# New orders at the ends of parts in a chain of two transformer blocks, and a conditioning product that ends eight blocks earlier

## The reference

```python
m_lat = jnp.split(cond_lat @ ada_w[i] + ada_b[i], 6, axis=-1)
h_lat = layer_norm(ALPHA * h_lat + m_lat[2] * y_lat, ln_g[i, 0], ln_b[i, 0])
f_lat = swiglu_2(modulate(h_lat, m_lat[3], m_lat[4]), ffn_w13[i], ffn_w2[i])
h_lat = layer_norm(ALPHA * h_lat + m_lat[5] * f_lat, ln_g[i, 1], ln_b[i, 1])
```

## Time and profile before

| | |
|---|---|
| Median of 3 runs | 2839.1 us (2837.92 to 2840.66) |
| The profiled execution: its own time | 2836.78 us |
| Its span, first to last instruction | 2835.0 us |
| Mean granted TensorE clock | 0.997 of full |
| PE busy | 2790.1 us, 98% |
| DVE busy | 1750.8 us, 62% |
| ACT, POOL busy | 1173.3 us (41%), 502.2 us (18%) |
| HBM read | 261.49 MB, 93 GB/s over the span |

### The profile page before, as it was taken

The page is one execution under the profiler, slowest core; times in us unless marked ns, Lnnn a source line. Parts: engine busy times, 40 slices in busy tenths (PEclk is TensorE's granted clock), DMA queues, the critical chain, the costliest instruction groups (busy, mean ns, idle before and its releaser), DMA issues.

```text
span 2835.0 us, 40815 instructions
## 1 busy us (share of the span) xinstructions
PE 2790.1 (98%) x16006; PEld 2449.7 (86%) x16006; DVE 1750.8 (62%) x3061; ACT 1173.3 (41%) x2064; POOL 502.2 (18%) x272
## 2 busy tenths in 40 slices
PE   9999999999999999999999999999999999999998
PEld 8888896988889888888888989999997778988888
DVE  7778688758795653544445896556675535633344
ACT  5332358642233641422424743334345555532222
POOL 2243300023332101111111000000012222122220
PEclk9999999999999999999999999999999999999999
DMA  6556412236654211121021012222223121133331
GB/s 207 183 186 193 148 63 90 75 110 218 187 193 124 83 45 60 38 67 45 31 86 48 17 62 76 71 68 64 79 68 101 49 75 66 53 112 104 97 97 38
DMA packets 86015, 267.81 MB, mean 94 GB/s; under 512 B 9152, under 2 KB 18752, under 8 KB 85568
## 3 DMA queue, kind: packets, MB, share of 16 engines
q1 hardware_dynamic: 85824, 265.20, 29.2%
HBM read 261.49 MB, written 2.10 MB: 93 GB/s over the span
## 4 chain that ended last, share of the span: by engine, by line
PE 92%; DVE 5%; ACT 1%; issue 1%; DMA 1%; SPq 0%; POOL 0%; DVEq 0%; ACTq 0%
PE ps L1986 29%; PE ps L1988 29%; PE ps L1987 29%; PE ps L2261 1%; PE ps L2245 1%; PE ps L2234 1%; DVE t_wlo L2661 1%; DMA t_x<-in_x 0%; PE ps L2125 0%; ACT t_whi L2303 0%; PE ps L2117 0%; PE ps L2176 0%; DVE t_m L2778 0%; PE ps L2189 0%; DVE t_hid L2905 0%
## 5 line engine op out<-in xcount | busy, mean ns | idle before, releaser
L1986 PE MATMUL ps<-t_h,t_whi 128*128 128x512 f32 (+2 forms) x2040 | 710.9, 348 | 3.6 <-DVE t_m L2980 1.3
L1987 PE MATMUL ps<-t_h,t_wlo 128*128 128x512 f32 (+2 forms) x2040 | 705.9, 346 | 0.0
L1988 PE MATMUL ps<-t_h,t_whi 128*128 128x512 f32 (+2 forms) x2040 | 705.7, 346 | 0.0
L2303 ACT CAST t_whi<-t_raw 128x1024 fp32r<-128x1024 f32 (+3 forms) x405 | 351.7, 875 | 580.5 <-PE ps L1988 446.3
L3272 POOL TENSOR_TENSOR t_wlo<-t_raw,t_whi 128x1024 fp32r<-128x1024 f32 (+3 forms) x130 | 292.6, 2251 | 1534.6 <-ACT t_whi L2303 1534.6
L1986 PE MATMUL ps<-t_hid,t_whi 128*128 128x256 f32 (+2 forms) x1336 | 436.1, 326 | 11.5 <-DVE t_hid L2711 6.1
L1987 PE MATMUL ps<-t_hid,t_wlo 128*128 128x256 f32 (+2 forms) x1336 | 433.1, 324 | 0.0
L1988 PE MATMUL ps<-t_hid,t_whi 128*128 128x256 f32 (+2 forms) x1336 | 432.5, 324 | 0.0
L1986 PEld LDWEIGHTS ps<-t_h,t_whi 128*128 128x128 f32 x2040 | 385.6, 189 | 51.7 <-issue 8.2
L1987 PEld LDWEIGHTS ps<-t_h,t_wlo 128*128 128x128 f32 x2040 | 385.7, 189 | 42.5 <-issue 1.2
L1988 PEld LDWEIGHTS ps<-t_h,t_whi 128*128 128x128 f32 x2040 | 385.5, 189 | 41.9
(11 more groups left out here) (344 smaller groups left out, 4671.9 us busy)
## 6 DMA issues: line engine op xcount, KB each, us to landing
t_raw<-in_gu SPq DMA_DIRECT2D x174, 512.0 KB, 3.3
t_raw<-in_ada SPq DMA_DIRECT2D x96, 512.0 KB, 3.7
t_raw<-in_dn SPq DMA_DIRECT2D x52, 512.0 KB, 3.7
t_raw<-in_dn SPq DMA_DIRECT2D x24, 384.0 KB, 3.4
t_raw<-in_ret_v SPq DMA_DIRECT2D x16, 512.0 KB, 3.3
t_raw<-in_ret_qk SPq DMA_DIRECT2D x16, 512.0 KB, 3.4
t_raw<-in_ret_g SPq DMA_DIRECT2D x16, 512.0 KB, 3.3
t_raw<-in_ret_o SPq DMA_DIRECT2D x16, 512.0 KB, 3.9
```

The source lines that it names most:

```text
L1986: e.matmul(out, whi, xlo, start=first, stop=False, skip_group_check=shared)
L1987: e.matmul(out, wlo, xhi, start=False, stop=False, skip_group_check=shared)
L1988: return e.matmul(out, whi, xhi, start=False, stop=last, skip_group_check=shared)
L2303: e.copy(m.block(0, it.slot, n), m.raw(it)).then_inc(*S["hi"].of(j))
```

## The change

Seven edits:

1. The order of the seven products becomes P1, P5, P6, P3, P7, P2, P4, and the order of the weight quadrants follows. S4 is now written to the place of S2 (in TMP) and not over A12, so it waits until S2's parts are made. The second half's up is issued before P4.
2. The down blocks of f3's parts 0 to 4 take the tokens 512 to 767 first, then 0 to 511. The last part takes SUB2 instead of SUB3, and the value rows start with the token tiles 4 and 5.
3. The events for the turned hidden values are split: the second half's serve tokens 512 on, the first half's tokens 0 to 511.
4. In f1, f2 and f4, the last four gate and up blocks of a part come as gate, gate, up, up.
5. `spread` deals the conditioning's rows over `places - 8`, so the last eight places get none.
6. `token_sums` no longer waits for the slots 9 and 10.
7. `mix_lambda` gets eight more `yield`s; `na_setup` waits for the roots of all three segments.

```diff
-QUADS = ("A11", "A12", "S2", "S1", "S3", "S4", "A22")
+QUADS = ("A11", "S1", "S2", "S4", "S3", "A12", "A22")
...
-        if q == "A12":
-            for name in ("S3", "S1", "S2", "S4"):
+        if q == "A11":
+            for name in ("S3", "S1", "S2"):
                 put("wadd", pid=pid, q=name, old=state["pair"])
             state["pair"] = pid
+        if q == "S2":
+            put("wadd", pid=pid, q="S4", old=None)
...
-                between((i + 1) * per // places - i * per // places)
+                between(min((i + 1) * per // (places - 8), per) - min(i * per // (places - 8), per))
...
+            if not halves:
+                specs[-3:-1] = specs[-2], specs[-3]
...
-                    token_sums(f, ver, halves, over_hid + gates[0] + closed[9] + closed[10])
+                    token_sums(f, ver, halves, over_hid + gates[0])
...
-                last = columns(specs, segs, between=spread)
+                last = columns(specs, segs[::-1] if halves else segs, between=spread)
...
                 los = [(f, pi, k, s) for s in ((0,), (1, 2))[half]]
                 if turned:
-                    los = los[:0] if half == 0 else [(f, pi, k, s) for s in range(3)]
+                    los = [(f, pi, k, s) for s in ((0, 1), (2,))[half]]
...
             product("P1", "A11", "B11", seat(banks["P1"], "drain_dve", (*key, "up", 0)))
             s1, keys1 = snap("P1")
+            product("P5", "S1", "T1", seat(banks["P5"], "drain_dve", (*key, "C12")))
+            s5, keys5 = snap("P5")
+            product("P6", "S2", "T2", [("snap", (*key, "P1"))])
+            s2, keys2 = snap("P6")
+            product("P3", "S4", "B22", [("snap", (*key, "P5"))])
...
+            product("P7", "S3", "T3", [("snap", (*key, "P6"))])
+            add("C22", "P5", s5, "P7", None)
             product("P2", "A12", "B21", seat(banks["P2"], "drain_dve", (*key, "C11")))
...
+            up(1, gate2, s5)
+            free(keys5, ("drain_dve", (*key, "up", 1)))
             product("P4", "A22", "T4", [("drain_dve", (*key, "C22"))])
             up(0, gate1, None)
-            up(1, gate2, s5)
-            free(keys5, ("drain_dve", (*key, "up", 1)))
...
-                rows([("na_v", 0, blk) for blk in range(4)], 6, pro, ("na_v", 0), lambda tt: NVV + vslot(tt) * 512, (0, 1, 2, 3, 4, 5), True)
+                rows([("na_v", 0, blk) for blk in range(4)], 6, pro, ("na_v", 0), lambda tt: NVV + vslot(tt) * 512, (4, 5, 0, 1, 2, 3), True)
...
-    ffn("f3", "gu3", "dn3", PARTS2, SEG2, SUB2, SUB3, 5, lambda pi: ("drain_dve", g3), None, whole=0, ahead=values_ahead, halves=384)
+    ffn("f3", "gu3", "dn3", PARTS2, SEG2, SUB2, SUB2, 5, lambda pi: ("drain_dve", g3), None, whole=0, ahead=values_ahead, halves=384)
...
-            done = e.tensor_tensor(q12, q12, s2, ALU.subtract)
+            done = e.tensor_tensor(s2, q12, s2, ALU.subtract)
...
         e.reciprocal(sp, den).then_inc(*then("sp"))
+        yield
         w.wait_ge("lru_dve", "sp")
...
         for k in (11, 9, 7, 5, 3, 1):
+            yield
             e.tensor_tensor(pl, pl, z, ALU.mult).then_inc(*then(("m", k)))
...
+        yield
         e.tensor_tensor(pl, pl, ratio, ALU.mult).then_inc(*then("pr"))
```

More of the change, by code:

```diff
@@ L972, in up @@
                 if turned:
-                    los = los[:0] if half == 0 else [(f, pi, k, s) for s in range(3)]
+                    los = [(f, pi, k, s) for s in ((0, 1), (2,))[half]]
                 it = dict(f=f, key=(*key, half), k=k, pitch=pitch, t0=half * n, n=n, slot=gate, source=source, off=off, over=over_hid,
-                          bank=banks["P4"], g=ids["P4"], los=los, turned=turned)
+                          bank=banks["P4"], g=ids.get("P4"), los=los, turned=turned)
                 put("seven_up", after=after, **it)
@@ L981, in seven_products @@
             s1, keys1 = snap("P1")
+            product("P5", "S1", "T1", seat(banks["P5"], "drain_dve", (*key, "C12")))
[3 more added lines that the diff above has]
+            product("P3", "S4", "B22", [("snap", (*key, "P5"))])
+            gate2 = gate_slot()
+            add("C12", "P6", s2, "P3", gate2, gates[gate2])
+            free(keys2, ("drain_dve", (*key, "C12")))
+            put("seven_silu", key=(*key, "C12"), slot=gate2, n=n)
+            gates[gate2] = [("drain_dve", (*key, "up", 1))]
+            product("P7", "S3", "T3", [("snap", (*key, "P6"))])
+            add("C22", "P5", s5, "P7", None)
             product("P2", "A12", "B21", seat(banks["P2"], "drain_dve", (*key, "C11")))
@@ L1435, in neighbourhood @@
             if half == 0:
-                late = pro + [("ps", ("root", "l01v", 2))]
+                late = pro + [("ps", ("root", "l01v", s)) for s in range(3)]
                 put("na_setup", after=late)
@@ L1621, in schedule @@
             raws[it.pid, it.which] = it.raw
-            it["last"] = [(it.pid + QUADS.index(q), low[it.pid + QUADS.index(q)]) for q in (("S3", "S4"), ("S1", "A22"))[it.which]]
+            it["last"] = [(it.pid + QUADS.index(q), low[it.pid + QUADS.index(q)]) for q in (("S4", "S3", "A12"), ("S1", "S2", "A22"))[it.which]]
         if it.kind == "wadd":
             it["raws"] = raws[it.pid, 0], raws[it.pid, 1]
-            it["taken"] = [("hi", it.old + 2), ("lo_dve", it.old + 2), ("wadd", (it.old, "S4"))] if it.old is not None else []
+            it["taken"] = [(name, it.old + QUADS.index("S4")) for name in ("hi", "lo_dve")] if it.old is not None else []
         if it.kind == "prep":
@@ L1695, in quad @@
     def quad(self, raw, q):
-        o = 512 if q in ("A12", "A22", "S4") else 0
-        if q == "S2":
+        o = 512 if q in ("A12", "A22") else 0
+        if q in ("S2", "S4"):
             return self.TMP[:, 2304:2816]
@@ L2679, in wadd @@
             w.wait_ge("wadd", (it.pid, "S2"))
-            w.wait_ge("hi", it.pid + 1)
-            w.wait_ge("lo_dve", it.pid + 1)
-            done = e.tensor_tensor(q12, q12, s2, ALU.subtract)
+            w.wait_ge("hi", it.pid + QUADS.index("S2"))
+            w.wait_ge("lo_dve", it.pid + QUADS.index("S2"))
+            done = e.tensor_tensor(s2, q12, s2, ALU.subtract)
         done.then_inc(*S["wadd"].of((it.pid, it.q)))
```

12 lines of the change are left out of this document (removed).

## The result

The changed kernel has a median of 2847.0 us (8 runs, 2846.2 to 2855.9), the kernel before 2839.3 (8 runs, 2836.8 to 2844.5). The ratio over all these runs is 1.0037, with a 95% interval of 1.0027 to 1.0047 (the two medians alone give 1.0027). Forecast were 2824.7, and 2835.0 at the most.

A forecast was written before the change was run, and what follows sets the result against it. PE, busy 98% of the span, was taken as the bound, losing time in stops and the half clock behind three. Gains of 20.9 us less 6.5 for f2's conditioning product gave 14.4 less, 2839.1 to 2824.7 us; range 2816.5 to 2835.

The forecast's parts named there:

- the same 6 more: f1: 6 more conditioning rows done by the end of a part, as in f2, covered by more weight slots; cost nothing.
- the ring's price: f2's part 1: each added load in the three raw buffers delays the next weight 2.4 us; 5.5 x 2.4 - 6.7 = 6.5 us.
- the upper bound in the text: f2's part 1: six added rows at DVE's full price of 3.4 us, less 6.7 us of cover, cost 13.7 us.
- the prediction's mechanism: f2's part 1: added loads use up 6.7 us of cover, weights' high and low parts come late, PE waits at block heads.
- stops that vanish: Ends of f1, f3's part 0 and f3's last part: half clock behind these stops goes too, gain 1.7 + 2.6 + 1.5 = 5.8 us.
- slower rival: f2's part 1: all halves beside POOL take 2.4 us, DVE falls behind, clock falls some 6 us; 2848 us, chance 0.04.
- 2.0 + 0.15 + 1.7: f1's end: the 2.0 us stop goes, with 0.15 us of slow restart and 1.7 us of half clock.
- 1.4 + 0.15: f2's end: 1.4 us gained from the 1.7 us stop, 0.25 staying, and 0.15 us of slow restart.
- The end of part 0: f3: the 3.7 us stop shrinks to 0.5 through earlier token sums and reversed down tokens; gain 3.2 us, half clock gone.
- The ends of parts 1 to 4 and of the last part: f3: four stops go through the new product order, gain 3.2 us; the last part's stop, third segment first, gain 2.9.
- The first pair: f3: PE's 1.2 us wait for a copy of P1 (L2308) nearly goes, gain 1.1 us; price between -1.1 and +2.05.
- estimate of 2.4 us for a half beside POOL: f2's part 1: a conditioning half beside POOL's work takes 1.22 + 0.46 / 0.39 = 2.4 us, against a 1.22 median.

The follow-up runs named there:

- base: The changed kernel with one edit taken back, the conditioning's rows dealt over all places again: 2822.5 us, ratio 0.9951 to the kernel before; measured again 2822.9.

## Why the prediction was wrong, point by point

**The cost of the conditioning's product was 24.5 us, not 6.5.** Three steps of it failed.

First, "f1 has the same 6 more (14.6 us at 2.4), but seven slots instead of four: 16 us more cover, so nothing". f1 cost 10.8 us. The sum of the slack was right: the low part of the first down block's weights ended 25 us ahead of its use before and 12 after. But the slots cover weights only. DVE goes through one list, and in it the drains of gates and ups stand between the halves. The lines of DVE around the stop, after (start, us, line):

```profile
203.59 0.68 DVE L2890 TENSOR_TENSOR t_m<-ps,t_tmp 128x512 f32<-128x512 f32 x1
204.20 1.21 DVE L2861 CUSTOM_DVE_ANT_0 t_m<-t_raw,t_m 128x1024 f32<-128x1024 f32 x1
205.34 0.08 DVE L2861 DVE_READ_ACCUMULATOR2_ANT t_mod<- 128x1 f32 x1
205.34 0.68 DVE L2890 TENSOR_TENSOR t_m<-ps,t_tmp 128x512 f32<-128x512 f32 x1
208.22 2.00 DVE L2665 TENSOR_TENSOR t_h<-t_raw,t_h 128x1024 fp32r<-128x1024 f32 x1 [2.20 <-ACT t_h L2307]
210.14 0.68 DVE L2903 TENSOR_TENSOR t_tmp<-t_m,ps 128x512 f32<-128x512 f32 x1
211.50 2.70 DVE L2909 TENSOR_TENSOR t_hid<-t_tmp,t_hid 128x512 fp32r<-128x512 f32 x1 [0.68 <-ACT t_hid L2415]
```

PE ended the part's last up at 201.4, and each block takes 5.44 us: the two gates that DVE drains at 203.6 and 205.3 ended three and two blocks earlier, at 185.1 and 190.5. DVE is 18 and 15 us late. PE doesn't feel it while it works on gates and ups, whose sums wait in PSUM; it feels all that is left of it at the part's end, where the down block needs the last hidden values. Even the 2.2 us for a weight's high part stand ahead of them, though PE takes up that weight only at 235.7. And the last L2909 shown takes 2.70 us, where most take 0.68: POOL's low part, which began first, runs from 211.32 to 213.65 (see the last section). Before, DVE waited for PE twice in that stretch and was up to date (its profile, same place):

```profile
195.23 0.69 DVE L2899 TENSOR_TENSOR t_tmp<-t_m,ps 128x512 f32<-128x512 f32 x1 [3.45 <-PE ps L1988]
...
201.41 0.69 DVE L2899 TENSOR_TENSOR t_tmp<-t_m,ps 128x512 f32<-128x512 f32 x1 [3.16 <-PE ps L1988]
```

The balance of DVE shows it. In 118 to 205 it is busy for 80.4 us after and waits 7.0 for conditioning loads, 87.4 of 87; before, the window and the group were:

```profile
118.00:205.00 87.00, 87.00 (x386) 72.06 (x385) 75.27 (x98) 27.75 (x33) 33.99 (x16) 1.00 0.64 200
```

```profile
L2857 DVE CUSTOM_DVE_ANT_0 t_m<-t_raw,t_m 128x1024 f32<-128x1024 f32 x33 | 50.5, 1565 | 4.8 <-DMA t_raw<-in_ada 4.8
```

80 of 87. The prediction looked at this balance for f2 only, and there used its waits for loads as idle time that more halves could fill.

Second, "I take the ring's price, and half a load as absorbed ... 6.5". f2 cost 13.7, the upper bound in the text, 6 x 3.4 - 6.7, to the tenth (by chance; the bound counted no clock). The right price was DVE's: cutting the loads to 1.9 us left 22 of the 24.5 us, cutting DVE's work took all of it, cutting POOL's 22. The slack ran out as the prediction's mechanism said, at the block that starts at 717.9, and the ring had its part in it: with short loads the 5.0 us of waits at 718, 731 and 750 are gone, as they also are with POOL's work cut. But of PE's waiting in this part 6.8 us are for weights (3.1, 1.8 and the 1.9 at 762.9, behind POOL's low part) and another 4.2 are for hidden values at the part's end, the same lateness as in f1, which had no term.

Third, new stops bring half clock. The prediction counted what goes with stops that vanish (5.8 us; measured, all three windows at full clock) and in its forecast nothing for those that come: about 2.7 us in f1 and 3.2 in f2. Only its slower rival had a term for them, 6 us.

**The slower rival named POOL, and the wrong condition.** It got 0.04, and the time landed 1 us below its 2848. That is luck: it put 30 us on f2's part 1, where f2 cost 13.7, had nothing for f1's 10.8, and counted gains of 20.9 where 14.5 came. It decides, the text said, once a mean half takes 2.1 us. The mean in f1's part 1 was 1.67, and in f2's stretch 1.53. Its reason against, that POOL is busy for 25 of 65 us only, was no reason: DVE needs no average of 2.1, only a sum over its part.

**The gains were 14.5 us, not 20.9** (base against before). By stages, in the second profile of base against that of before: f1 3.9 (forecast 2.0 + 0.15 + 1.7), f2 1.1 (forecast 1.4 + 0.15; a stop of 0.6 us stays at its end, 1.2 in the first profile), f3 9.9 against 15.6.

The number for f1 is right, its reason is not shown. The kernel with neither the swap nor the pieces has 3.2 of the 3.9 us, by the other order of DVE told above. And single profiles differ here: base's first has 1.7, with a stretch of half clock at 34 us that the kernel before doesn't have. In f2 the swap does count: without it and the pieces 0.2 of the 1.1 us is left.

Of f3 three terms:

- The end of part 0 keeps 1.1 us of 3.7, where 0.5 was left over, but its half clock is gone, as forecast. The cover comes from the tokens alone; "the sums can run while DVE is idle" was no part of it.
- The ends of parts 1 to 4 and of the last part are free of stops, 3.2 + 2.9 as forecast. The reason given for the last part (the third segment comes first) was half of it: with the old products its 2.9 us stay.
- The first pair was to gain 1.1 and loses about 3 in the changed kernel. There PE waits 1.9 us for L2695, 1.4 for L2665 (the low part of a weight quadrant) and 0.8 for L2312 (a copy), 4.1 us for the 1.2 of the earlier trace rows. That is past its price range of -1.1 to 2.05: not the weight alone (1.4) but also the sum C22 (L2695), which P4 waits for with DVE full of token sums, and the copy, which did not go away.

## What to carry to other kernels

Before work on an in-order engine is packed closer, add up its list over the part, waits for loads included, and compare with the part's length; a buffer of weights covers weights, not the drains that stand in the same list. Lateness is free in the middle of a part and is paid in full where its last value is needed, and here half the packing cost an eighth of the whole. Two orders that look like separate edits can be one: try them apart, since the smaller alone may lose. And where a planner orders the whole program, a gain of the forecast size at the forecast place is no proof of its reason: take the edit back and look whether the gain goes.

## What the runs showed of the hardware

A half of the conditioning's product takes 1.21 us or up to 3.45. In the part of the trace that holds f1 and f2, 43 of the changed kernel's 192 halves take over 1.4 us, and 58 before, and every one of them ends 1.08 or 1.09 us after the end of a POOL instruction. One case, DVE's rows first, then POOL's:

```profile
178.96 3.45 DVE L2861 CUSTOM_DVE_ANT_0 t_m<-t_raw,t_m 128x1024 f32<-128x1024 f32 x1 [1.62 <-DMA t_raw<-in_ada]
182.34 0.08 DVE L2861 DVE_READ_ACCUMULATOR2_ANT t_mod<- 128x1 f32 x1
182.34 2.30 DVE L2861 CUSTOM_DVE_ANT_0 t_m<-t_raw,t_m 128x1024 f32<-128x1024 f32 x1
```

```profile
178.94 2.39 POOL L3279 TENSOR_TENSOR t_wlo<-t_raw,t_whi 128x1024 fp32r<-128x1024 f32 x1 [9.11 <-ACT t_whi L2307]
181.28 2.28 POOL L3285 TENSOR_TENSOR t_m<-t_m,t_tmp 128x512 f32<-128x512 f32 x1
```

By that distance the half does nothing until 181.33, when POOL's first ends; it ends 1.08 later, at 182.41. The profile books the wait as busy time. POOL's second, 1.3 us when alone, takes 2.28, since it stands behind the half; the next half ends 1.08 us after it. So the two engines don't slow each other by a share: one holds the other out for a whole instruction. The Trainium skill (SBUF — State Buffer, SBUF: two separate sides) calls this port pair an exclusive lock that the instruction which starts first keeps to its end; the trace agrees in all 101 cases. The prediction's estimate of 2.4 us for a half beside POOL was good: the halves over 1.4 us take 2.4 on average in its stretch of f2 and 2.5 over both traces. The price of a half is thus set by where in POOL's instruction it starts, and it is POOL's time, in pieces, that DVE's list pays for. The same shows in DVE's other instructions that read two tiles in SBUF. In the changed kernel's whole trace 27 of the L2909 are long (up to 2.9 us where one of 512 columns takes 0.68), and they end 0.55 us after the end of a POOL instruction (0.28 with 256 columns); 8 of the L2665 are, and they end 1.08 or 1.09 us after one. Among them are the L2909 at 211.50 and at 769.10, on which the stops of 8.6 and 2.9 us end.

How far a stop brings half clock could not be told from its length. In the changed kernel it came with the stops that end at 214, 763 and 774 (8.6, 1.9 and 1.4 us) and not with those that end at 718, 731, 750 and 772 (1.1 to 2.9 us); in base a stop of 1.9 us in f3's first pair has a window of half clock behind it in one profile and none in the other. What a new stop costs is read from the window behind it, counted from the product with which PE starts again.
